# Attention's turned probabilities and value products one or two slots later, token rows fetched first, one SSD sigmoid moved, the last output quarter by token halves

## What is computed

```
for l in range(2):                                  # first block
    h = rmsnorm(x, norm_mix[l]);  proj = h @ w_in[l]
    p = softmax(q k^T * scale + bias);  o = p @ v     # 32 heads of width 64
    x = x + concat(rmsnorm(o_a), rmsnorm(o_b), rmsnorm(o_c)) @ w_o[l]
    x = x + relu(rmsnorm(x) @ w_up[l])**2 @ w_down[l]
...                                                 # norm_final, LRU and mLSTM layer
z, xbc, dt = split(rmsnorm(x, o_norm) @ w_in)       # SSD layer, 8 groups of 8 heads
xs, b, c = split(silu(causal_conv(xbc)))
y = rmsnorm((ssd_scan(xs, dt, a, b, c) + d_skip * xs) * silu(z), gnorm)   # norm by group
x = x + y @ w_out
return rmsnorm(x, final_norm)
```

## Time and profile before

| | |
|---|---|
| median of three runs | 3571.8 us |
| profiled execution, its span | 3574.1 us, 3572.3 us |
| mean granted TensorE clock | 0.995 |
| TensorE matmuls | 3504.6 us busy, 98% of the span |
| VectorE, ScalarE, GpSimd | 62%, 45%, 17% |
| DMA | 618 MB, mean 173 GB/s |
| first transpose of x; first weight matmul | 13.74 us; 21.97 us after the span's start |
| last weight matmul starts | 3560.72 us |
| the fourth store is issued | 3568.99 us |

### The profile page before, as it was taken

How to read it: one execution, slowest core, us unless ns; L and a number is a source line. 1 busy time by engine, 2 the same in 40 slices (tenths; PEclk the granted TensorE clock), 3 DMA queues, 4 the chain that set the end, 5 groups by cost and what they waited for, 6 DMA issues and landing times.

```text
span 3572.3 us, 45011 instructions
## 1 busy us (share of the span) xinstructions
PE 3504.6 (98%) x18462; PEld 2912.5 (82%) x18462; DVE 2225.8 (62%) x2152; ACT 1597.9 (45%) x1764; POOL 589.7 (17%) x528
## 2 busy tenths in 40 slices
PE   7999999999999999999999999999999999999998
PEld 6777888888887777888888878888888888788886
DVE  5667646464655666646464658866576575775676
ACT  4555433333344555434343445633444444553553
POOL 1231000000000221000000001650000079540540
PEclk9999999999999999999999999999999999999999
DMA  6444555555555344555555544455444454345443
GB/s 208 142 153 160 181 188 187 188 189 188 187 183 190 133 165 150 184 187 188 188 188 188 199 177 165 179 188 186 156 143 153 164 183 174 140 154 188 161 159 140
DMA packets 89887, 618.45 MB, mean 173 GB/s; under 512 B 10256, under 2 KB 12560, under 8 KB 16496
## 3 DMA queue, kind: packets, MB, share of 16 engines
q1 hardware_dynamic: 83952, 601.99, 47.1%
q0 software_dynamic: 3168, 11.41, 1.0%
q10 hardware_dynamic: 2592, 2.55, 0.2%
HBM read 613.75 MB, written 2.10 MB: 172 GB/s over the span
## 4 chain that ended last, share of the span: by engine, by line
PE 90%; DVE 4%; ACT 2%; issue 1%; DMA 1%; POOL 1%; DVEq 0%; SPq 0%; ACTq 0%; POOLq 0%
PE ps L2272 27%; PE ps L2274 14%; PE ps L2230 7%; PE ps L2231 7%; PE ps L2232 7%; PE ps L2328 2%; PE ps L2685 2%; PE ps L2686 2%; PE ps L2687 2%; PE ps L2304 2%; PE ps L2305 1%; PE ps L2306 1%; DVE wlo L1374 1%; PE ps L2367 1%; PE ps L2369 1%
## 5 line engine op out<-in xcount | busy, mean ns | idle before, releaser
L2272 PE MATMUL ps<-act,whi 128*128 128x512 f32 x4384 | 1551.1, 396 | 1.9 <-DVE wlo L1367 1.8
L2274 PE MATMUL ps<-act,wlo 128*128 128x256 f32 x4384 | 1233.7, 281 | 0.0
L1367 DVE TENSOR_TENSOR wlo<-raw,whi 128x2048 fp32r<-128x2048 f32 x404 | 941.2, 2350 | 468.0 <-ACT whi L926 445.8
L2272 PEld LDWEIGHTS ps<-act,whi 128*128 128x128 f32 x4384 | 824.1, 188 | 202.8 <-issue 8.4
L926 ACT ACTIVATE whi<-raw 128x2048 fp32r<-128x2048 f32 x358 | 683.6, 1913 | 616.6 <-DMA raw<-in_w_down 309.9
L2274 PEld LDWEIGHTS ps<-act,wlo 128*128 128x128 f32 x4384 | 822.8, 188 | 0.5
L818 ACT ACTIVATE whi<-raw 128x2048 fp32r<-128x2048 f32 x212 | 404.4, 1913 | 279.0 <-DMA raw<-in_o_w_in 113.8
L1374 DVE TENSOR_TENSOR wlo<-raw,whi 128x2048 fp32r<-128x2048 f32 x166 | 393.4, 2374 | 160.4 <-ACT whi L818 160.4
L2230 PE MATMUL ps<-whi,act 128*128 128x512 f32 x1152 | 455.7, 396 | 0.0
L2231 PE MATMUL ps<-wlo,act 128*128 128x512 f32 x1152 | 455.2, 395 | 0.0
L2232 PE MATMUL ps<-whi,act 128*128 128x512 f32 x1152 | 455.1, 395 | 0.0
(11 more groups left out here) (393 smaller groups left out, 4502.8 us busy)
## 6 DMA issues: line engine op xcount, KB each, us to landing
raw<-in_w_up SPq DMA_DIRECT2D x128, 1024.0 KB, 4.8
raw<-in_w_down SPq DMA_DIRECT2D x128, 1024.0 KB, 4.8
raw<-in_o_w_in SPq DMA_DIRECT2D x80, 1024.0 KB, 4.8
raw<-in_e_w_in SPq DMA_DIRECT2D x64, 1024.0 KB, 4.8
raw<-in_w_in SPq DMA_DIRECT2D x60, 1024.0 KB, 4.8
raw<-in_w_o SPq DMA_DIRECT2D x32, 1024.0 KB, 4.8
raw<-in_e_w_out SPq DMA_DIRECT2D x32, 1024.0 KB, 4.8
raw<-in_o_w_out SPq DMA_DIRECT2D x32, 1024.0 KB, 4.8
```

Source lines behind the costliest of these rows:

```text
L1367: dve.tensor_tensor(wlo[:, slot, :], raw[:, slot, :], whi[:, slot, :].bitcast(F32), ALU.subtract).then_inc(sem("lo_ready"), 1)
L2272: pe.matmul(ps[:, b + f, :], whi[:, slot, w], a[:, kt, :, :].rearrange("p a t -> p (a t)"), start=(kt == 0), stop=False)
L2274: ins = pe.matmul(ps[:, b + f, S:2 * S], wlo[:, slot, w], a[:, kt, 0, :], start=False, stop=(kt == KT - 1))
```

## The change

- Attention's turned probabilities move from S + 5 to S + 6 for p < 8 and to S + 7 for the rest, and everything that follows them on TensorE, ScalarE and VectorE with them. `turned_probs` comes ahead of `exps` within a slot, and `softmax_sum` ahead of `low_unit`. The sums move from slots 110, 137, 163 to 111, 139, 165; `KA_TURN` stays.
- At the start x's first quarter comes ahead of weight unit 0, the second ahead of unit 1. GpSimd waits for all of x before it issues the tables. The first unit is split in two halves, with the second turned piece of x between them. ScalarE runs one tiny Copy at once, and TensorE runs 5 matmuls of ones before x and 6 after its first transposes. VectorE waits for the constants at slot 12 only.
- In the SSD stages 0 and 1, `conv_sigmoid(11)` and `z_sigmoid(0)` move from the end of stage 0 to behind `y_squares(0)` in stage 1.
- The last output quarter goes by (token half, column block) pairs in `OUT_ORDER`; the first token half is normed, scaled and stored while the second is multiplied. Of the second half GpSimd multiplies three quarters by the gain row, ScalarE scales half and VectorE the rest.

```diff
-        SUMS_AT = [110, 137, 163]
+        T_AT = [t + 6 for t in S_AT[:8]] + [t + 7 for t in S_AT[8:]]
+        V_AT = [t + 3 for t in T_AT]
+        SUMS_AT = [111, 139, 165]
...
+        OUT_ORDER = [(0, 0), (0, 1), (0, 2), (1, 0), (0, 3), (1, 1), (1, 2), (1, 3)]
...                                                  (SyncE)
-            weight_unit(first_gemm, 0, 0, 0)
             for c in range(4):
                 for th in range(2):
                     sp.dma_start(x[:, th, 512 * c:512 * c + 512], A["x"][0, th * P:th * P + P, 512 * c:512 * c + 512]
                                  ).then_inc(sem(f"x_dma{c}"), 16)
-                if c == 0:
-                    weight_unit(first_gemm, 0, 0, 1)
+                if c < 2:
+                    weight_unit(first_gemm, 0, 0, c)
...
+                    for c in range(2):
+                        sp.wait_ge(sem("out_low"), c + 1)
+                        store(0, slice(1024 * c, 1024 * c + 1024))
+                    sp.wait_ge(sem("out_high"), 1)
+                    store(1, slice(0, 1024))
+                    for c in range(2):
+                        sp.wait_ge(sem("out_low"), c + 3)
+                        store(1, slice(1024 + 512 * c, 1536 + 512 * c))
...                                                  (GpSimd)
+                    pool.wait_ge(sem("x_dma3"), 32)
                     rope_tables(0)
...
+                    for p in range(3):
+                        pool.wait_ge(sem("x_sq1"), p + 1)
+                        cols = slice(512 * p, 512 * p + 512)
+                        pool.tensor_tensor(x[:, 1, cols], x[:, 1, cols], gain_row[:, cols], ALU.mult
+                                           ).then_inc(sem("out_gained"), 1)
...                                                  (ScalarE)
+                    act.activation(osum[:, 0:1], ones[:, 0:1], ACT.Copy)
...
                         turned_high(0, s["turned"], X0)
+                        act.wait_ge(sem("raw0"), 16)
+                        act.activation(whi[:, 0, 0:1024], raw[:, 0, 0:1024], ACT.Copy).then_inc(sem("hi_first"), 1)
                         turned_high(1, s["turned"], X0)
-                        high_unit(U)
+                        act.activation(whi[:, 0, 1024:2048], raw[:, 0, 1024:2048], ACT.Copy).then_inc(sem("hi_ready"), 1)
...
+                        if t - 1 in T_AT:
+                            turned_probs(T_AT.index(t - 1))
                         if t - 1 in S_AT:
                             exps(S_AT.index(t - 1))
-                        if t - 6 in S_AT:
-                            turned_probs(S_AT.index(t - 6))
-                        if t - 9 in S_AT:
-                            mixed(S_AT.index(t - 9))
+                        if t - 1 in V_AT:
+                            mixed(V_AT.index(t - 1))
...
+                    if g == 1:
+                        y_squares(0)
+                        conv_sigmoid(11)
                     high_unit(u + 3)
-                    if ended:
+                    if g == 1:
+                        z_sigmoid(0)
+                        z_sigmoid(1)
+                    elif ended:
                         z_sigmoid(2 * g - 1)
                         y_squares(g - 1)
...
                     conv_sigmoid(10 + 2 * g)
-                    conv_sigmoid(11 + 2 * g)
-                    z_sigmoid(2 * g)
+                    if g:
+                        conv_sigmoid(11 + 2 * g)
+                        z_sigmoid(2 * g)
...
+                    for n, (th, p) in enumerate(OUT_ORDER):
+                        act.wait_ge(sem("evacuated"), s["G0"] + n + 1)
+                        (square of x[:, th, block p]; after block 3 of a half, the root of its sum)
+                    act.wait_ge(sem("out_rstd"), 2)
+                    act.wait_ge(sem("out_gained"), 2)
+                    act.activation(x[:, 1, 0:1024], x[:, 1, 0:1024], ACT.Copy, scale=rs[:, 2, 1:2]
+                                   ).then_inc(sem("out_high"), 1)
...                                                  (VectorE)
+                        if t - 3 in S_AT:
+                            softmax_sum(S_AT.index(t - 3))
                         if t % 4 == 1:
                             low_unit(U + t // 4 + 2)
...
-                        if t - 3 in S_AT:
-                            softmax_sum(S_AT.index(t - 3))
-                        if t - 10 in S_AT:
-                            mixed_low(S_AT.index(t - 10))
+                        if t - 2 in V_AT:
+                            mixed_low(V_AT.index(t - 2))
...
+                    low_unit(u + 14)
+                    add_rows(0)
+                    add_rows(1)
+                    low_unit(u + 15)
+                    for n in range(2, 5):
+                        add_rows(n)
+                    dve.wait_ge(sem("gain_row"), 32)
+                    row_scale(0)
+                    scaled_out(0, slice(0, 1024))
+                    add_rows(5)
+                    scaled_out(0, slice(1024, 2048))
+                    add_rows(6)
+                    add_rows(7)
+                    row_scale(1)
+                    dve.wait_ge(sem("out_gained"), 3)
+                    dve.tensor_scalar(x[:, 1, 1024:1536], x[:, 1, 1024:1536], rs[:, 2, 1:2], None, ALU.mult
+                                      ).then_inc(sem("out_low"), 1)
+                    scaled_out(1, slice(1536, 2048))
...                                                  (TensorE)
-                        if t - 5 in S_AT:
-                            turn_probs(S_AT.index(t - 5))
-                        if t - 8 in S_AT:
-                            head_values(S_AT.index(t - 8))
+                        if t in T_AT:
+                            turn_probs(T_AT.index(t))
+                        if t in V_AT:
+                            head_values(V_AT.index(t))
...
                     if l == 0:
+                        for n in range(5):
+                            pe.matmul(ps[:, 7, 0:P], ones[:, :], ones[:, :], start=True, stop=True)
                         pe.wait_ge(sem("ident_in"), 16)
                         pe.wait_ge(sem("x_dma0"), 32)
                         turn_raw(0, X0)
                         turn_raw(1, X0)
+                        for n in range(6):
+                            pe.matmul(ps[:, 7, 0:P], ones[:, :], ones[:, :], start=True, stop=True)
...
+                    for i, (th, p) in enumerate(OUT_ORDER):
+                        (waits: parted, evacuated of the same bank, lo_ready of unit 12 + p; then 12 matmuls, rows_done)
```

More of the change, by code:

```diff
@@ L2131, in _, with add_rows, row_scale, scaled_out @@
                     low_unit(u + 13)
-                    for p in range(4):
+                    def add_rows(n):
+                        th, p = OUT_ORDER[n]
+                        dve.wait_ge(sem("rows_done"), n + 1)
                         dve.wait_ge(sem("parted"), 2 * p + 2)
-                        add_block(p, u + 13 + p, sem("evacuated"))
-                        if p < 2:
-                            low_unit(u + 14 + p)
+                        xs = x[:, th, 512 * p:512 * p + 512]
+                        dve.tensor_tensor(xs, ps[:, 2 * ((s["G0"] + p) % 2) + th, :], xs, ALU.add
+                                          ).then_inc(sem("evacuated"), 1)
+                    def row_scale(th):
+                        dve.wait_ge(sem(f"x_sq{th}"), 4)
+                        dve.tensor_reduce(rs[:, 0, th:th + 1], ss[:, th, :], AX.X, ALU.add).then_inc(sem("out_sum"), 1)
+                        dve.wait_ge(sem("out_std"), th + 1)
+                        dve.reciprocal(rs[:, 2, th:th + 1], rs[:, 1, th:th + 1]).then_inc(sem("out_rstd"), 1)
+                        dve.wait_ge(sem("out_rstd"), th + 1)
+                    def scaled_out(th, c):
+                        dve.scalar_tensor_tensor(x[:, th, c], x[:, th, c], rs[:, 2, th:th + 1], gain_row[:, c],
+                                                 ALU.mult, ALU.mult).then_inc(sem("out_low"), 1)
+                    low_unit(u + 14)
[16 more added lines that the diff above has]
+                    scaled_out(1, slice(1536, 2048))
                 T.done(**counts(s))
@@ L2295, in wide_part @@
                         slot, b = u % SLOTS, bank(k)
-                        pe.wait_ge(sem("lo_ready"), u + 1)
+                        pe.wait_ge(sem("lo_ready") if u else sem("lo_first"), u + 1)
                         for a in range(4):
                             kt = 4 * n + a
+                            if u == 0 and a == 2:
+                                pe.wait_ge(sem("lo_ready"), 1)
                             if k == 0 and kt % 2 == 0:
@@ L2745, in _ @@
                     done = {}
-                    for i, (p, n) in enumerate(passes(s)):
+                    for i, (p, n) in enumerate(passes(s)[0:12]):
                         u, b = 2 * s["G0"] + i, 2 * ((s["G0"] + p) % 2)
-                        first, last = n in (0, 3), n in (2, 3)
```

(25 more changed lines are left out.)

40 lines of the change are left out of this document (23 added, 17 removed).

## The result

The changed kernel takes 3538.6 us, the median of four runs (3535.3 to 3539.0), against 3573.2 us for the kernel before on the same chip: a ratio of 0.990, 95% interval 0.989 to 0.991. That is 34.6 us, 1.0%. Forecast were 39.9 us and 3532 us, with a range of 3525 to 3546. The profiled execution took 3538.9 us, 3537.1 of them in its span; TensorE is busy for 99% of it.

A forecast was written before the change was run, and what follows sets the result against it. TensorE, busy 98%, was taken as the bound, so only its waits and clock could gain: 11.0 start + 17.9 attention + 8.5 SSD + 2.5 end = 39.9 us, giving 3534.2 profiled, 3532 us median; range 3525 to 3546.

The forecast's parts named there:

- Attention: Both attention layers: waits before the transposes of the probabilities (14.5 us) and two half-clock stretches (3.4 us) go, 17.9 us gained.
- Rival (c): Attention: ScalarE's weight rounding ahead of the copies becomes the bound at 12 steps, 3605 us, slower; chance 0.03.
- `exps` wait a little longer: Attention: the exponentials wait for the transposes at most 1 us against 1.4 us given; counted as nothing.
- Rival (d): Attention: the deferral does nothing because every wait moves along with TensorE's slots, 3550 us; chance 0.02.
- The start: Kernel start: TensorE begins near 10 us, is held until 25.3 to 28.4 instead of 37.47; 11.0 us gained.
- the square of x precedes its rounding but fits in before unit 3 lands: Start, ScalarE: squaring x adds no delay before weight unit 3 lands, at 20.3 to 23.4 us.
- (b): Start bounded by TensorE alone: tables cost nothing, resumption at 23 us, 14.5 us gained there, 3528 us; chance 0.10.
- The SSD: SSD layer: the 6.76 us wait before the squares' sums and its half-clock loss go, less a new wait; 8.5 us gained.
- The term for the new wait: SSD: `ssd_bases` wait 1.3 us for GpSimd's gates, too short for the clock to fall.
- The end: Output: shorter work after the last matmul, last issue near 3566.6 instead of 3569.0 us; 2.5 us gained.
- the time from there to the end of the span, 3.3 us, stays: Output: from the last store's issue to the end of the span still takes 3.3 us.
- The prediction's bound of 2.7 us: TensorE's clock: it falls after a wait of 2.7 us or more, costing 1.7 us.

The follow-up runs named there:

- e2: The kernel before with attention's later slots alone, ScalarE and VectorE keeping the old order inside a slot: 3584.1 us.
- e1: The kernel before with the whole attention part of the change alone: 3550.3 us, ratio 0.993.
- e11: The kernel before with the later slots and `turned_probs` ahead of `exps`, `softmax_sum` still behind the weight split: 3550.2 us.
- e6: The changed kernel with VectorE's activation split in SSD stage 1 held until GpSimd's convolution is done: 3539.3 us.
- e9: The changed kernel with VectorE's activation split in SSD stage 1 held until GpSimd has written both gates: 3536.6 us.
- e4: The changed kernel without GpSimd's wait for all of x, so the tables of constants are issued at once: 3541.7 us.
- e10: The changed kernel with x's fifth and sixth pieces ahead of weight unit 3 and without the matmuls of ones: first scores at 96.44 us, whole time not given.
- e3: The kernel before with the new order inside a slot alone, transposes and value products staying at S + 5 and S + 8: 3568.1 us.
- e5: The changed kernel without TensorE's matmuls of ones: 3532.9 us.

## Why the prediction was right, and where its steps were wrong

**What bounds the kernel**: right. Everything gained is waits and clock of TensorE.

**Attention**, 17.9 forecast, 23.3 measured. Waits and clock went in full: 14.5 + 3.4. Mis-sized is what a stop costs beyond its wait. By the starts of the matmuls around it, a stop costs 0.16 us more than the bracket shows (the hold of 2.44 us above moved the next start by 2.60): 16 stops, 2.6 us. That makes 20.5 of the 23.3. The transposes, without the waits, took 27.0 us from start to start for 256, before 29.2, but these 2.2 us are in the sum already: 13 of them stood in the two halved stretches (1.6 us) and six came just ahead of a stop between the two heads of a pair (1.0 us). The 2.8 us that are left come in small amounts at single steps. Some are holds too short for the list: at the fifth pair of layer 0 the first transpose started 0.45 us after the matmul ahead of it, and 0.24 us at the next two pairs. I did not follow the rest. Rival (c), ScalarE ahead of the copies, had 0.03, and in the changed kernel it fell. But e2 shows that its mechanism is real, and one call's place away: I priced it at the roundings, which are ready, and never asked what the exponentials, the other work that could stand ahead of the copies, wait for. The sentence "`exps` wait a little longer" named the order and missed its weight. Rival (d) fell with e1 and e11.

**The start**, 11.0 forecast, 7.1 measured. The shape was right, and the profiled pair shows a bad draw (8.4 us on the mean): first weights at 12.19 us (forecast 10), a hold on the fifth piece until 28.83 us (forecast 25.3 to 28.4), 8.6 us ahead there and not 9.1 to 12.2. The step that failed is "the square of x precedes its rounding but fits in before unit 3 lands": it began at 21.77, unit 3 landed at 22.74, and ScalarE was free at 23.67. Then came 1.9 + 2.3 us and the first piece, as said. x itself came at 7.3 us, not at 4.9 to 5.5: the DMA moved 285 GB/s from 2 to 7.3 us, not the 364 that I took, and it had moved some 1.5 MB by then, not 0.9. So data issued behind it (weight unit 0 at 2.12 us, the next quarter of x at 2.60) came in along with the first quarter, which I had put strictly first. The second failed step is the clock: I let it fall after 2.7 us or more; it fell after 2.44 us and cost the next 1.5 us. The rivals' start, bounded by TensorE alone (b), fell with it.

**The SSD**, 8.5 forecast, 4.4 measured. `y_sums` began without a wait (3018.01), as forecast. The term for the new wait was 1.3 us; it was 3.0 with 3.4 us of halved clock behind it, 1.7 + 1.7 us, and e6 and e9 name the cause: VectorE, no longer held by ScalarE, ran its split beside GpSimd. I looked for what was late next in the lists, not for what would now run at the same time. A further 0.6 us went with a wait of 0.5 us for a later split (L2347, at 3053.1 us), of the kind that the prediction had in its range. (The end of `y_sums`, 3049.0 in the prediction, is 3049.14 by its own rows.)

**The end**, 2.5 forecast, 1.7 measured. The 0.9 us for unit 13 came as said (0.875). The last issue is at 3533.0, 4.7 us after the last matmul's start, not 5.7; the terms that I listed for it add up to 3565.3 and not to the 3566.6 that I wrote, so this sum was wrong by 1.3 us before any run. But "the time from there to the end of the span, 3.3 us, stays" failed: it is 4.1 us. The last three pieces, 1 MB, are issued within 0.9 us, from 3532.16 on, where before the stores went out over 3.6 us:

```profile
3532.16 1.64 SPq L643 DMA_DIRECT2D out<-x  x3
```

GpSimd's multiplies took 1.29, 1.51 and 1.29 us, not 1.02, and were hidden.

**Between attention and SSD** I had nothing; 1.3 us were lost, about half of them to a wait of 1.6 us (L2686) in place of shorter ones.

## What to carry to other kernels

When a step is moved to a later slot, list what now shares its slot on each in-order engine, and ask of each call ahead of it what it waits for: here the order of two calls on ScalarE decided between 5.8 us lost and 23.3 us gained. When a stall goes, ask what the freed engine will now run beside, not only what is late next; a VectorE split beside GpSimd took 3.4 us of the SSD term, a later place in the lists 0.6. A hold near the start makes everything spent to start TensorE faster worthless, so remove the hold first and then warm the engine.

## What I had not expected of the chip

**The clock after a wait is not decided by the wait's length alone.** I went through all waits of TensorE over 1.2 us in the fourteen traces, without those ahead of its first weight matmul. Up to 1.77 us the clock never fell behind them (25 waits), and from 3.3 us on it always did. Between these it fell after 14 waits, of 1.84 us (e2, SSD), 2.0 us (e2, both layers), 2.25 us (e4), 2.44 us (after) and more up to 2.98 us. But it did not after 2.77 us (e9), 2.94 us (e10) and 2.96 us (e4), and e3 has the same wait of 2.33 us in both layers, with the clock falling in one. The hold at the start in e9, with the stretch behind it, and the bases' wait in e4 with its stretch:

```profile
28.14 0.47 PE L2383 MATMUL ps<-whi,act 128*128 128x512 f32 x1 [2.77 <-DVE act L1566]
...
28.10:36.00 7.90, 7.86 (x38) 6.51 (x39) 6.25 (x11) 6.26 (x9) 0.00 (x0) 1.00 0.25 86
```
```profile
3026.09 0.67 PE L2243 MATMUL ps<-wide_a 128*128 128x256 f32 x2 [2.96 <-issue]
...
3026.09:3033.00 6.91, 6.91 (x43) 6.18 (x44) 6.10 (x8) 3.84 (x4) 5.60 (x5) 1.00 0.00 0
```

So between 1.8 and 3.0 us either was seen, and a fall costs up to 1.7 us; what decides it I did not establish. The prediction's bound of 2.7 us came from too few waits. e9's wait of 1.47 us is below all that were followed by a fall; but e4 kept its clock there with 2.96 us, so that gain of clock is not certain to be the edit's.

**A stretch that runs 1.3% faster by chance.** In the LRU and mLSTM layer, at the same granted clock, e5 started 862 matmuls in 150 us and the changed kernel 851 (its window above, e5's below):

```profile
2320.00:2470.00 150.00, 150.00 (x851) 130.72 (x850) 95.96 (x76) 60.25 (x45) 27.49 (x23) 1.00 0.52 186
```
```profile
2318.00:2468.00 150.00, 150.00 (x862) 131.38 (x861) 98.02 (x77) 59.44 (x45) 26.60 (x23) 1.00 0.54 190
```

A product of 512 columns followed the last by 230.0 ns in e3 and e5 and by 233.2 to 233.9 in the twelve others, with the same instructions. With a wait that is shorter behind it, this gave e5 3.6 us and e3 3.0 us that have nothing to do with their edits. Why, stays open. It is the best reason here to judge edits of a few us by events near them and not by the end.
